# Down-projection weights stored by column halves, and a reordered way into the first mixer

## The reference, cut to what matters

```python
def expert_choice_ffn(h, w_router, w_gate, w_up, w_down):
    ...                                     # every expert takes the 32 rows that fit it best
    xe = jax.vmap(lambda hb, ib: hb[ib])(h, idx)
    a = jax.nn.silu(jnp.einsum('becd,edf->becf', xe, w_gate)) * jnp.einsum('becd,edf->becf', xe, w_up)
    ye = jnp.einsum('becf,efd->becd', a, w_down) * gate[..., None].astype(h.dtype)
    y = jax.vmap(lambda yb, ib: jnp.zeros((seq, d), yb.dtype).at[ib.reshape(-1)].add(yb.reshape(-1, d)))(ye, idx)
    return y
...
x = x + expert_choice_ffn(h2, w_router[l], w_gate[l], w_up[l], w_down[l])
...
# second block, layer 0
shift, scale, gate = jnp.split(jax.nn.silu(c) @ ada_w + ada_b, 3, axis=-1)
hn = rmsnorm(h, norm_g) * (1.0 + scale) + shift
u = hn @ s5_w_in                            # then the S5 scan, w_glu, w_out, gate, a conv FFN,
...                                         # a forgetting-attention layer and a second conv FFN
```

## Time and profile before

| what | value |
|---|---|
| runs shown | 1316.57 us median of three (1311.68 to 1319.81) |
| the profiled execution | 1316.12 us, span 1314.3 us |
| PE busy | 1191.1 us (91% of the span) |
| PEld busy | 851.7 us (65%) |
| DVE busy | 669.4 us (51%) |
| ACT busy | 462.2 us (35%) |
| POOL busy | 168.1 us (13%) |
| moved by DMA | 371.81 MB, 283 GB/s on average |
| experts' weights | 96 loads of 2048 KB, 23.7 to 25.7 us from issue to landing in the median |

### The profile page before, as it was taken

The page is one execution under the profiler, slowest core; times in us unless marked ns, Lnnn a source line. Parts: engine busy times, 40 slices in busy tenths (PEclk is TensorE's granted clock), DMA queues, the critical chain, the costliest instruction groups (busy, mean ns, idle before and its releaser), DMA issues.

```text
span 1314.3 us, 22196 instructions
## 1 busy us (share of the span) xinstructions
PE 1191.1 (91%) x8874; PEld 851.7 (65%) x8874; DVE 669.4 (51%) x1207; ACT 462.2 (35%) x746; POOL 168.1 (13%) x270
## 2 busy tenths in 40 slices
PE   8999899887789877787999999999999989999996
PEld 5646554432335323332877889999969767999995
DVE  3677452231211221121486757676675766667675
ACT  5463421010100001002654454444455545443343
POOL 0000115572343032101020000000000000000000
PEclk9999899898987899798999999999999999999998
DMA  9865599999999999999786465555456241554441
GB/s 372 356 222 244 230 404 418 430 428 428 428 428 428 428 429 428 429 428 428 291 349 231 161 272 203 181 191 191 176 193 240 82 160 49 187 192 184 178 178 40
DMA packets 38389, 371.81 MB, mean 283 GB/s; under 512 B 4133, under 2 KB 7742, under 8 KB 14398
## 3 DMA queue, kind: packets, MB, share of 16 engines
q1 hardware_dynamic: 34462, 365.47, 68.8%
q10 hardware_dynamic: 3872, 5.57, 1.2%
HBM read 369.94 MB, written 1.08 MB: 282 GB/s over the span
## 4 chain that ended last, share of the span: by engine, by line
PE 66%; DMA 23%; DVE 5%; ACT 3%; issue 2%; POOL 1%; DVEq 0%; SPq 0%; ACTq 0%
PE ps L705 64%; DMA ring<-in_w_up 20%; DMA ring<-in_ada_w 2%; PE ps L936 1%; DMA ring<-in_fox_out 1%; DMA ring<-in_s_out 1%; ACT XH L1617 1%; DVE X L2774 1%; DVE ring_parts L516 1%; ACT XH L1575 0%; PE ps L712 0%; DVE W L2955 0%; DMA X<-in_x 0%; PE ps L948 0%; DVE XH L2773 0%
## 5 line engine op out<-in xcount | busy, mean ns | idle before, releaser
L705 PE MATMUL ps<-W_parts 128*128 128x256 f32 (+2 forms) x2672 | 383.9, 305 | 3.9 <-DVE W_parts L2898 2.0
L705 PEld LDWEIGHTS ps<-W_parts 128*128 128x128 f32 x2672 | 356.8, 191 | 28.0 <-issue 4.1
L705 PE MATMUL ps<-ring,W 128*32 128x512 f32 (+2 forms) x1512 | 239.3, 679 | 55.2 <-DMA ring<-in_w_up 29.1
L705 PEld LDWEIGHTS ps<-ring,W 128*32 128x32 f32 (+1 forms) x1512 | 62.1, 124 | 190.8 <-issue 114.6
L705 PE MATMUL ps<-W 128*32 128x64 f32 (+7 forms) x1696 | 135.6, 290 | 23.9 <-DVE W L2755 12.8
L705 PEld LDWEIGHTS ps<-W 128*32 128x32 f32 (+5 forms) x1696 | 85.6, 152 | 78.3 <-issue 70.8
L2743 DVE COPY W<-ps 128x1024 f32<-128x1024 f32 x16 | 19.6, 1224 | 191.4 <-PE ps L705 191.4
L2856 DVE TENSOR_TENSOR W_parts<-ring,W_parts 128x2048 fp32r<-128x2048 f32 x44 | 100.8, 2292 | 26.2 <-ACT W_parts L1942 26.0
L705 PEld LDWEIGHTS ps<-kc,W 128*128 128x128 f32 x648 | 85.7, 212 | 28.2 <-DVE W L2743 17.4
L705 PE MATMUL ps<-kc,W 128*128 128x32 f32 (+2 forms) x648 | 88.1, 293 | 10.2 <-DVE W L2743 9.4
L705 PE MATMUL ps<-XH_parts,ring_parts 128*128 128x256 f32 x512 | 94.0, 286 | 2.1 <-ACT XH_parts L1578 1.9
(11 more groups left out here) (395 smaller groups left out, 1353.5 us busy)
## 6 DMA issues: line engine op xcount, KB each, us to landing
ring<-in_w_up SPq DMA_DIRECT2D x32, 2048.0 KB, 25.7
ring<-in_w_down SPq DMA_DIRECT2D x32, 2048.0 KB, 23.7
ring<-in_w_gate SPq DMA_DIRECT2D x29, 2048.0 KB, 24.0
ring<-in_ada_w SPq DMA_DIRECT2D x24, 2048.0 KB, 10.1
ring<-in_up SPq DMA_DIRECT2D x44, 1024.0 KB, 5.8
ring<-in_dn SPq DMA_DIRECT2D x44, 512.0 KB, 3.3
ring<-in_fox_in SPq DMA_DIRECT2D x6, 2048.0 KB, 7.9
ring<-in_w_o SPq DMA_DIRECT2D x2, 2048.0 KB, 15.7
```

The costliest lines, as they stand in the source:

```text
L705: return pe.matmul(o, l, r, start=a, stop=z_, skip_group_check=True, **kw)
```

## The change

Four things change.

1. On the host, `w_down` is cut by columns: j = 4 holds all 1024 contraction rows of the columns 0 to 511, j = 5 those of the columns 512 to 1023. `down(n)` multiplies one such half into bank 5 + n only. PE's order becomes `down(0)`, scatter of the first column half (two matmuls into the banks 0 and 1), `down(1)`, scatter of the second (banks 2 and 3). ACT's copy of bank 5 waits for j = 4 only; DVE's copy of bank 6 still for j = 5, and its additions run in the order of the banks.
2. Behind the last expert, PE transposes ahead of `ada_product(8)`, and `ada_product(9)` moves behind `features("s5",0)`.
3. ACT does the table load first and squares in three pieces of 512 columns as the additions deliver them; the fourth piece is squared by DVE (`tensor_tensor_reduce`), and one DVE instruction adds the partial sums of both row tiles.
4. The first quarter of the split work (half 0 of s5_in 0) leaves ACT: POOL now makes the high part too (a cast), and then subtracts as before. `w_high` counts one less from there on.

```diff
@@ weights split
-            eng.wait_ge(S("w_high"), 2 * n + half + 1)
+            eng.wait_ge(S("w_high"), 2 * n + half)
@@ PE, one expert
+                def down(n):
+                    w = filled("expert", 4 + n, i * 2 + b).rearrange("p (c n) -> p c n", c=NC)
+                    for c in range(NC):
+                        last = mm(ps[32 * (c % 4):32 * (c % 4) + 32, 5 + n, :], aT[:, c, :], w[:, c, :], c < 4, c >= 4,
+                                  tile_position=(0, 32 * (c % 4)))
+                    last.then_inc(S("expert_mm"), 1)
+                def scatter(n):
+                    pe.wait_ge(S(f"y{n}_copied"), at(1, 1))
+                    for t in range(NT):
+                        mm(ps[:, 2 * n + t, :], ScT[:, t * P:t * P + P], Ys[:, BANK * n:BANK * n + BANK],
+                           True, True).then_inc(S("scatter_mm"), 1)
...
-                for j in range(4, 6):
-                    grouped(j, aT[:, 4 * (j % 2):4 * (j % 2) + 4, :], 5, j == 4)
+                down(0)
                 if early:
                     rest(7 if b else 4, 4)
                     pe.wait_ge(S("xe_copied"), 15 if b else 12)
                 pe.wait_ge(S("sct_copied"), at(1, 1))
                 if tabled:
                     pe.wait_ge(S("kc_copied"), i + 1)
-                pe.wait_ge(S("y0_copied"), at(1, 1))
-                pe.wait_ge(S("y1_copied"), at(1, 1))
-                for t in range(NT):
-                    for n in range(2):
-                        mm(ps[:, 2 * n + t, :], ScT[:, t * P:t * P + P], Ys[:, BANK * n:BANK * n + BANK],
-                           True, True).then_inc(S("scatter_mm"), 1)
+                scatter(0)
+                down(1)
                 if early and b == 0:
                     rest(5, 5)
+                scatter(1)
@@ PE, behind the experts
-            ada_product(8)
             turn(1, 0)
             turn(1, 1)
-            ada_product(9)
+            ada_product(8)
             first_ready(1)
             features("s5", 0, XNr, s5l, (4, 5), "u_mm", turned=1)
+            ada_product(9)
             ada_product(10)
             features("s5", 1, XNr, s5l, (6, 3), "u_mm")
             ada_product(11)
@@ ACT
-                act.wait_ge(S("expert_mm"), at(6, 6))
+                act.wait_ge(S("expert_mm"), at(6, 5))
                 act.activation(Ys[:, 0:BANK], ps[:, 5, :], ACT.Copy).then_inc(S("y0_copied"), 1)
...
-            apart_high(act, 0, (0,))
             warmed()
-            row_squares(1, 0, None, "x_added", 4 * NE + 2)
-            for n in range(2):
-                row_squares(1, 1, n, "x_added", 4 * NE + 3 + n)
+            for t, n in ((0, 0), (1, 0), (0, 1)):
+                row_squares(1, t, n, "x_added", 4 * NE + 2 * n + t + 1, 2 * n + t)
@@ POOL
-            apart_low(pool, 0, 0)
+            pool.wait_ge(filled_sem[slot_of["s5", 0]], filled_at("s5", 0))
+            own(pool.tensor_copy(ringr[:, high_slot["s5", 0], 0:SLOT // 2],
+                                 ring[:, slot_of["s5", 0], 0:SLOT // 2]))
+            tt(ringr[:, slot_of["s5", 0], 0:SLOT // 2], ring[:, slot_of["s5", 0], 0:SLOT // 2],
+               ringr[:, high_slot["s5", 0], 0:SLOT // 2].bitcast(F32), ALU.subtract).then_inc(S("w_low0"), 1)
@@ DVE
+                if r == 2:
+                    v.wait_ge(S("squares"), 3 * (r - 2) + 5)
+                    last = stt(ss[:, 0:NT], ss[:, 0:NT], EPS, ss[:, NT:2 * NT], ALU.add, ALU.add)
...
-                for j, k in enumerate((0, 2, 1, 3)):
-                    v.wait_ge(S("scatter_mm"), at(4, j + 1))
+                for k in range(4):
+                    v.wait_ge(S("scatter_mm"), at(4, k + 1))
...
             v.wait_ge(S("x_added"), 4 * NE + 4)
+            own(v.tensor_tensor_reduce(normed_rows[1][:, 1, BANK:D], X[:, 1, BANK:D], X[:, 1, BANK:D], 1.0 / D, 0.0,
+                                       ALU.mult, ALU.add, ss[:, 3:4]))
             both_halves(1, 2, 0, XNr, s5l)
@@ host
-        "w_gate": halves(a["w_gate"][0]), "w_up": halves(a["w_up"][0]), "w_down": halves(a["w_down"][0]),
+        "w_gate": halves(a["w_gate"][0]), "w_up": halves(a["w_up"][0]), "w_down": column_halves(a["w_down"][0]),
+    def column_halves(w):
+        return w.reshape(NE, NC, P, 2, -1).transpose(0, 3, 2, 1, 4).reshape(NE * 2, P, -1)
```

12 lines of the change are left out of this document (7 added, 5 removed).

## The result

| | before | changed |
|---|---|---|
| median | 1316.57 us (7 runs, 1311.68 to 1319.81) | 1323.41 us (7 runs, 1320.15 to 1332.10) |
| ratio | 1 | 1.0059, 95% interval 1.0034 to 1.0083 |
| the profiled execution | 1316.12 us, span 1314.3 us | 1320.15 us, span 1318.4 us |

The forecast was 1318.0 us, from 1312 to 1323. The change costs 7.8 us by the ratio where 2.0 were forecast. The median is 0.4 us above the range; that it would stay within one per cent of before, the case called same, came true. The profiled execution of the changed kernel was the shortest of its seven and shows only 4.1 us more span than the profile of before, so one pair of profiles doesn't hold the whole loss. All kernels in this document compute the whole reference.

A forecast was written before the change was run, and what follows sets the result against it. The prediction took DMA bytes to bound the expert loop and a PE, ACT and DVE chain the rest. Early experts 1.2 plus `bu(0)` 0.8 made +2.0 us on 1316.12, thus 1318.1, stated as 1318.0, range 1312 to 1323.

The forecast's parts named there:

- What bounds the kernel: Expert loop bound by DMA bytes at 428 GB/s; behind the last expert, a chain through PE, ACT and DVE.
- Rival (c): Expert loop: added pauses lower PE's clock until PE becomes the bound, slower beyond measure; chance 0.02.
- Part 1, in experts 0 and 1: Early experts: additions no longer hidden delay product 0 and leave DMA engines idle, +1.2 us, bounds 0 and 2.1.
- Part 1, the last expert: Tail behind the last weights: the extra wait costs as much as two matmuls save, last addition +0.8 us.
- Part 2, from the last addition to `features`: Way into the mixer: root 1.8 us earlier, features start 2.4 us earlier with the tail's +0.8 included.
- hidden: POOL's cast and subtraction on s5_in 0: done by 624.7 at the latest, ahead of features at 627.4.
- rival (d): Way into the mixer: POOL's operations twice as long as the bound, 6.4 us behind features' start, 1324 us; chance 0.02.
- Part 2, what is late next: Behind features: ada 9's place and s_glu 0 landing behind ada 11 delay `bu(0)`, +0.8 us, between -0.1 and +1.6.
- (a): Whole change: all gained, nothing lost, early loads covered and s_glu 0 in time, 1314 us; chance 0.25.
- (b): Whole change: early-expert and `bu(0)` losses both whole, 2.1 + 1.6 = 3.7, 1319.8 us; chance 0.18.

The follow-up runs named there:

- three against three: Three profiles each of the changed kernel and the kernel before, one execution each, compared by landmarks: difference of the mean spans +8.0 us.
- the second profile: The changed kernel profiled once more with nothing edited, one execution: span 1322.7 us.
- experiment 4: Changed kernel with ada product 9 back ahead of features(s5,0): 1321.50 us, ratio 1.0040 to before.
- experiment 3: Changed kernel with both down products ahead of both scatter halves: 1325.22 us, ratio 1.0069 to before.
- experiment 8: Changed kernel, both down products ahead of the scatters, ada 9 ahead of features, POOL's subtraction behind DVE's sum of squares: 1320.14 us, ratio 1.0013 to before.
- experiment 11: Changed kernel, both scatters behind both down products, ada 9 ahead of features, DVE subtracting instead of POOL: 1314.66 us, ratio 0.9979 to before.
- experiment 5: Changed kernel with POOL's subtraction waiting behind DVE's sum of the squares: 1325.90 us, ratio 1.0065 to before.
- experiment 9: Changed kernel with the subtraction given to DVE, POOL only casting: 1324.27 us, ratio 1.0060 to before.
- experiment 12: Kernel before with one edit, ada product 9 moved behind features(s5,0): 1321.29 us, ratio 1.0031 to before.
- experiment 13: As experiment 12, with s_glu 0 ahead of ada 11 in SP's list: 1319.17 us, ratio 1.0026 to before.
- experiment 14: As experiment 9, with s_glu 0 ahead of ada 11 in SP's list: 1320.11 us, ratio 1.0022 to before.
- experiment 10: Changed kernel with the old experts, ada 9 ahead of features, and DVE subtracting instead of POOL: 1316.26 us, ratio 0.9998 to before.

## Why the prediction was wrong, step by step

**What bounds the kernel** was right: 428 GB/s in the loop and PE waiting there, the end set behind it by the chain through PE, ACT and DVE. Rival (c) didn't come. (Its some 40 us per expert at half speed are 42 by the granted 0.87, 24 x 0.87 x 2; nothing hangs on it.)

**Part 1, in experts 0 and 1**: +1.9 us from the first load to s_in 0 in three against three, forecast +1.2 with 2.1 as the bound. Mechanism and place were right: product 0 of expert 1 waits for the additions now, at 198.39, 1.74 us later, of which 0.7 were in the start (forecast 1.2), and the DMA engines idle where they should. The second scatter half began 22.3 us behind the `w_gate` load, forecast 22.4, though the 1.5 us in that step of the prediction come from no row. Over all profiles the term is less sure: w_gate to s_in 0 took 441.0 to 445.1 us in eight with the old experts (median 441.7) and 442.8 to 444.3 in nine with the new (median 443.6).

**Part 1, the last expert** was mis-sized: +0.8 forecast, +2.6 measured. I went through the tail with durations at the old mixture of clocks: `down(0)` to end at 610.8, as the old j = 4 product did. It ended at 614.6. Of these 3.8 us, 2.05 are the later s_in 0 of that profile, and 1.65 the transposing sums ahead of `down(0)`, which took 3.62 us at the lower clock (1.97 in before). `down(0)` itself took 3.37, about what the old j = 4 product took, also at the lower clock. From its start to the end of the last addition it is 11.5 us, in before 10.5: 1.0 more, where 0.8 were forecast. So the extra wait was sized well, and the clock ahead of it was the miss. In the second profile the slow pieces were `down(0)` with 3.64 and the first scatter half with 3.75 us (1.95 in the first). The granted clock of the 12 us that end 3 us ahead of the end of the last addition was 0.58 to 0.73 in eight of nine profiles with the new experts (0.86 in experiment 4, whose tail is 2.73 us), and 0.72 to 0.86 in eight with the old ones (tails 2.3 to 3.8). So the tail is long where PE runs at 1.2 GHz for much of it, and it did so more often with the halves. Why is not shown: experiments 3 and 8 put PE's work together and had 1.00 and 0.86, but experiment 11, built in nearly the same way, had 0.59 and a tail of 6.96 us.

**Part 2, from the last addition to `features`**: root forecast 1.2 us behind the end of the last addition, measured 2.0 to 2.3, and up to 4.6 in experiment 4 and 5.5 in 3. The step that failed is the price of DVE's square "as its addition, 0.69", together with calling POOL "hidden". The addition has one input in PSUM; the square has both in SBUF, and POOL's subtraction held it. In rival (d) I had the rule on the shared interfaces before me, but asked only what it does to POOL, which had time, and never what POOL does to the one DVE instruction on the path. With it the root stood 7.35 us behind s_in 0 (7.3 also at the tails of 2.73 and 3.74 us), where the prediction had 4.3 (620.0 against 615.7); without it the changed kernel's own tails of 5.1 to 5.4 us and the 1.0 us of experiments 5 and 9 would give 6.1 to 6.4. So this step alone accounts for the whole miss of 3.0 us up to the root, and the longer tail alone for 1.8 to 2.1 of it. The row that I took for proof (617.65 to 622.17) proves nothing of the kind. DVE did very little beside it: the end of one addition out of PSUM, two instructions on one column, and the start of a reciprocal of two columns, each with one input in SBUF. Its row scaling began only behind POOL's end. The kernel before:

```profile
620.39 0.15 DVE L2244 TENSOR_SCALAR ss<-ss 128x1 f32<-128x1 f32 x1 [2.38 <-ACT W L1555]
...
621.53 0.21 DVE L2243 TENSOR_SCALAR ss<-ss 128x1 f32<-128x1 f32 x1 [0.99 <-ACT W L1555]
...
622.27 0.88 DVE L2254 TENSOR_SCALAR W<-X,rs 128x512 f32<-128x512 f32 x2
```

Everything else of this part came as put: 7.4 us from root to features, and the full clock in `features` (11.5 us, at the better end of the two). In all the part gave -2.8 us where -4.05 were forecast.

**Part 2, what is late next** was right, piece by piece: s_glu 0 lands 13.1 us after its issue (forecast 13.4), ACT stands at that split, `bu(0)` waits for ACT, and from the end of `features` it takes 18.6 to 18.8 us (forecast 19.2, before 15.2). Experiments 4, 12, 13 and 14 confirm it: 1.7 us for the product, 1.5 to 2.0 for the list. Only the balance was off, since the gain that was to pay for it came to 2.8 us.

**The sum** was short by two things more. The start ahead of the change cost 2.2 us in the three profiles, which no step had. The same time varies from 169.5 to 177.5 us over all profiles taken, while nothing of an edit has executed: 1.00 granted between 145 and 177 went with 169.5 (experiment 10), 0.84 with 173 to 174, 0.73 with 176.7. All six profiles above 176 us have the new way into the mixer, and the six with the old one lie between 172.7 and 174.9; that is too few to tell. Whether the 2.2 us are chance or something that the changed kernel brings stays open. And 0.7 us were added behind `bu(0)`. Together: 2.0 forecast, + 0.7 (early idle) + 1.8 (tail) + 1.2 (root and features) - 0.5 (`bu(0)`) + 2.2 (start) + 0.7 = 8.1, against 8.0 measured.

**The range** reached 1323 for (a), (b) and the spread of three runs. It held no case in which a term of the tail doubled by the clock, though the earlier trace rows has both levels in it. By its own rule the low end would be 1309 (1314 less 4.9) and not 1312.

**Still open**: why experiment 10's 3 us don't reach the time. From `bu(0)` to the conv FFN the profiles take 112.6 to 120.5 us, tied to no edit; experiment 12 with 120.5 had PE at 0.74, 0.91 and 0.83 between 660 and 720, the first profile of before 1.00 in each. A gain of 3 us can drown there, but it wasn't shown that it does.

## What to carry to other kernels

Before work goes to an idle POOL, list DVE's instructions on the path beside it by where their inputs lie: here those with two inputs in SBUF, and a scaling of 512 columns from SBUF to SBUF, waited for the end of POOL's instruction, a cast as well as a subtraction; those with an input in PSUM, and one-input instructions on one or two columns, didn't. Moving an instruction also moves the release of a buffer, and in a strict list of loads the next load is behind that release: the plan of the loads is to be moved with it. Two causes can put the same instruction at the same time, and then mending one brings little or nothing: count from an event that lies ahead of both. Where a short chain runs at either of two clocks, cost it at both, and compare segments between landmarks from several profiles before one pair of spans is believed.

## What the runs showed of the hardware

POOL's subtraction (two inputs in SBUF, 4.5 us) held DVE until its own end: the square of 512 columns took 0.69 us alone and 1.65 to 1.94, 3.26 and 4.26 beside it, by how much of the 4.5 us was left, and ended each time 0.55 us behind POOL's end; an addition of two columns took 0.16 and 4.33; two row scalings 0.88 and 4.81. Beside POOL's cast (1.89 us, one input) the square took 1.03 in experiments 3 and 8 and ended 0.54 us behind the cast. DVE's additions with one input in PSUM took 0.68 to 0.69 in all cases. Nor were small instructions with one input in SBUF held: 0.15 and 0.21 us for one column, 0.17 for a reciprocal of two. It may go the other way too: the one subtraction of POOL that took 4.82 us (experiment 3; 4.51 to 4.55 elsewhere) began while DVE's square was under way. The Trainium skill (SBUF — State Buffer, SBUF: two separate sides) calls the shared port pair an exclusive lock, held for the whole instruction, the other side fully blocked. The trace agrees: in experiment 5 POOL's 4.51 us ended at 629.10, the first of DVE's two scalings 0.28 us behind that, and the second, which takes 0.47, at 629.78.
